# Delta-rule layer: tables by each head's half of the array, v kept on chip, and a scan that loads two chunks at a time

## The reference, cut to what matters

```python
r, k, v = heads(xr @ wr), heads(xk @ wk), heads(xv @ wv)
decay = heads(exp(-exp(w)))
kk = k * k_k;  kk = kk / max(norm(kk), 1e-12)
k = k * (1 + (a - 1) * k_a)
def step(S, (r_t, w_t, k_t, v_t, a_t, b_t)):        # a = -kk, b = kk * a
    sa = einsum('bhij,bhj->bhi', S, a_t)
    S = S * w_t + sa * b_t + v_t * k_t               # outer products over i, j
    return S, einsum('bhij,bhj->bhi', S, r_t)
S, y = scan(step, S0, ...)                           # S0: zeros (prompt), state_rwkv (stream)
y = groupnorm(y) * ln_w + ln_b + sum(r * k * r_k) * v    # the last term: the "bonus"
```

## Time and profile before

| | us |
|---|---|
| median of 3 runs | 4401.09 (4398.41 to 4402.56) |
| execution profiled, its own time | 4410.82 |
| its span | 4409.1 |
| TensorE busy (share of the span) | 3709.2 (84%) |
| VectorE busy | 1550.3 (35%) |
| ScalarE busy | 1213.5 (28%) |
| GpSimd busy | 573.6 (13%) |

### The profile page before, as it was taken

How to read it: one execution, slowest core, us unless ns; L and a number is a source line. 1 busy time by engine, 2 the same in 40 slices (tenths; PEclk the granted TensorE clock), 3 DMA queues, 4 the chain that set the end, 5 groups by cost and what they waited for, 6 DMA issues and landing times. The chain is left out here.

```text
span 4409.1 us, 58432 instructions
## 1 busy us (share of the span) xinstructions
PE 3709.2 (84%) x24411; PEld 3469.6 (79%) x24411; DVE 1550.3 (35%) x2413; ACT 1213.5 (28%) x2151; POOL 573.6 (13%) x812
## 2 busy tenths in 40 slices
PE   4889473699799999998978979387498699999998
PEld 3689361498699999998567969377398599999998
DVE  3310133532433223233414654554532333223233
ACT  2421223430232112122523432165330232112123
POOL 0000030010011001012202123433010021001011
PEclk7989686899899999999889988699799899999999
DMA  3322201012121111111544554587412211111111
GB/s 111 130 82 68 89 14 42 13 53 97 46 57 44 48 45 47 48 43 39 193 142 135 188 162 130 134 163 132 96 48 92 59 40 47 49 44 48 47 43 62
DMA packets 546227, 349.26 MB, mean 79 GB/s; under 512 B 244294, under 2 KB 509414, under 8 KB 542550
## 3 DMA queue, kind: packets, MB, share of 16 engines
q1 hardware_dynamic: 539830, 328.31, 26.4%
q0 software_dynamic: 6144, 17.34, 1.2%
HBM read 246.82 MB, written 98.85 MB: 78 GB/s over the span
## 5 line engine op out<-in xcount | busy, mean ns | idle before, releaser
L79 PE MATMUL ps<-ff_h,ff_wh 128*128 128x352 f32 x4224 | 1009.6, 322 | 0.0
L79 PEld LDWEIGHTS ps<-ff_h,ff_wh 128*128 128x128 f32 x4224 | 731.4, 188 | 1.3
L79 PE MATMUL ps<-y_parts,ff_wh 128*128 128x352 f32 x2880 | 702.7, 326 | 16.3 <-DVE ff_wl L1512 16.3
L79 PE MATMUL ps<-ff_h,ff_wl 128*128 128x352 f32 x2112 | 677.6, 321 | 0.0
L79 PEld LDWEIGHTS ps<-y_parts,ff_wh 128*128 128x128 f32 x2880 | 506.8, 190 | 16.6 <-DVE ff_wl L1512 16.6
L79 PE MATMUL ps<-y_parts,ff_wl 128*128 128x352 f32 x1440 | 469.3, 326 | 0.0
L79 PEld LDWEIGHTS ps<-ff_h,ff_wl 128*128 128x128 f32 x2112 | 396.4, 188 | 0.0
L79 PE MATMUL ps<-rw_parts,tb_wh 128*128 128x352 f32 (+1 forms) x1152 | 298.6, 342 | 82.0 <-DVE tb_wl L1512 28.2
L1656 DVE TENSOR_TENSOR x<-ps,x 128x352 f32<-128x352 f32 x240 | 126.0, 525 | 495.7 <-PE ps L79 493.1
L1889 POOL TENSOR_TENSOR ff_silu<-ff_silu,rs 128x352 f32<-128x352 f32 x132 | 126.3, 958 | 1234.8 <-ACT ff_silu L1828 1234.8
L79 PEld LDWEIGHTS ps<-rw_parts,tb_wh 128*128 128x128 f32 x1152 | 210.5, 199 | 92.4 <-DVE tb_st L2718 29.0
(11 more groups left out here) (407 smaller groups left out, 5859.4 us busy)
## 6 DMA issues: line engine op xcount, KB each, us to landing
ff_w<-in_ffn_w SPq DMA_DIRECT2D x120, 512.0 KB, 3.8
mixed_t<-oq_st SPq DMA_DIRECT2D x48, 176.0 KB, 1.8
rw_ra_d<-tb_ra SPq DMA_DIRECT2D x8, 1056.0 KB, 6.6
rw_kbt_d<-tb_kbt SPq DMA_DIRECT2D x8, 1056.0 KB, 3.9
rw_gg_d<-tb_gs SPq DMA_DIRECT2D x8, 1056.0 KB, 5.5
mk_w<-in_xa_wk SPq DMA_DIRECT2D x4, 2048.0 KB, 9.0
mk_w<-in_xa_wv SPq DMA_DIRECT2D x4, 2048.0 KB, 9.4
oq_w<-in_xa_wq SPq DMA_DIRECT2D x16, 512.0 KB, 4.1
```

The costliest lines, as they stand in the source:

```text
L79: mm = nc.tensor.matmul(out, l, part, start=start and n == 0, stop=stop and n == 2)
```

## The change

Tables:
- The weights' buffers (`Groups`) are made outside of both stages. SyncE loads units 0 and 1 in `low_ranks`, ScalarE rounds them after `bend_g(0)`, VectorE makes the low parts at the end. `low_ranks` has five stage slots instead of six and one buffer `low` instead of two.
- `kb` has 64 columns instead of 128: no zeroed copies. Each cross product is made twice, for the partitions 0 to 63 and 64 to 127 as rows and outputs, with the weights' 64 columns. `turn` does the same with `V`, which lies whole in SBUF, two pairs deep; `eye2` goes.
- `bonus` is one operation from V in SBUF for a whole pair, a step later, and TensorE doesn't wait for it. `beta` is loaded pair by pair.
- The ring of mixed tiles has ten places (`RING`).
- DRAM layouts of triangles and of v follow the heads' halves; v is stored in four copies a pair.

Scan: one block for prompt and stream, the stream's chunk first, all eight pairs in one piece for each operation. A load brings two chunks; kbt, v and tt are used as loaded; only g and ra are opened (four operations). x comes back behind the second load.

```diff
+RING = 10
     def cross(p, i):
-                for k in range(c0, c1):
-                    mm = nc.tensor.matmul(ps[:, 6, (k - c0) * HD:(k - c0 + 1) * HD], kb[:, k, :], eye2[:], start=True,
-                                          stop=True)
+                for k in range(c0, c1):
+                    for r in (slice(0, HD), slice(HD, P)):
+                        mm = nc.tensor.matmul(ps[r, 6, (k - c0) * HD:(k - c0 + 1) * HD], kb[r, k, :], ident[r, r],
+                                              start=True, stop=True)
...
-            def open_kb(q, which, of):
-                for h in range(2):
-                    nc.vector.scalar_tensor_tensor(out=kb[:, :, (2 * which + h) * C:(2 * which + h + 1) * C], in0=by_c(of),
-                                                   scalar=of_key[:, h:h + 1], in1=by_c(ei), op0=ALU.mult, op1=ALU.mult)\
-                        .then_inc(kb_done, 1)
+            def grown_key(which, of):
+                nc.vector.tensor_tensor(kb[:, :, which * C:(which + 1) * C], by_c(of), by_c(ei), ALU.mult)\
+                    .then_inc(kb_done, 1)
...
-                    if u >= 1:
-                        pe.wait_ge(bonus_done, 4 * (u - 1) + (1, 2, 4)[b])
                     groups.sum(pe, j, b, parts, 0, KT // 2)
...
+            def bonus(u):
+                dve.wait_ge(beta_in[u % 2], 32 * (u // 2 + 1))
+                dve.wait_ge(bonus_out, 16 * u)
+                for b in range(BLOCKS):
+                    groups.wait_emptied(dve, 2 * KT + u, b)
+                nc.vector.tensor_tensor(extra, V[:, u % 2], A[:, u % 2], ALU.mult).then_inc(bonus_done, 1)
...
+                if u >= 1:
+                    bonus(u - 1)
+                for _ in range(min(8, C - 1 - done) if 2 <= u < 6 else 8 if u >= 6 else 0):
+                    substitute(dve, nc.vector, 0, 0, share, done // (C - 1), done % (C - 1))
```

SyncE's side of the new scan:

```diff
+            sp.wait_ge(cleared, 2)
+            for l in range(NPC // 2 + 1):
+                if l >= 2:
+                    sp.wait_ge(y_done, last(l - 2) + 1)
+                w = 2 if l else 1
+                c = 2 * (l - 1) if l else NPC
+                s, got = l % 2, two_in[l % 2]
+                for t, d in ((g_in, g_d), (ra_in, ra_d), (kbt, kbt_d)):
+                    sp.dma_start(t[:, s, :, 0:w, :], d[:, :, c:c + w, :].rearrange("p r c x -> r p c x")).then_inc(got, 16)
+                for h in range(2):
+                    sp.dma_start(v[h * HD:h * HD + C, s, :, 0:w, :],
+                                 vt_d[:, h * C:(h + 1) * C, c:c + w, :].rearrange("p s c x -> s p c x")).then_inc(got, 16)
+                for q in range(2):
+                    for h in range(2):
+                        for odd in range(2):
+                            r = odd * HD + h * C
+                            for sub in range(w):
+                                sp.dma_start(tt[r:r + C, s, sub, 2 * q:2 * q + 2, h, C:HD],
+                                             tt_d[q, c + sub, h, odd].rearrange("p s t -> s p t")).then_inc(got, 16)
+                if l == 1:
+                    sp.dma_start(x[:], x_d.rearrange("(k p) t -> p k t", p=P)).then_inc(x_in, 16)
```

TensorE's (chunk n is half `sub` of load `l`; `last(l)` = 2 l):

```diff
+            def open_z(n):
+                (l, sub), s = two(n), n % 2
+                pe.wait_ge(opened, OPENS * (n + 1))
+                if n >= 2:
+                    pe.wait_ge(z_out, n - 1)
+                z_part(n, lambda p: g[:, s, p, 0], lambda p: v[:, l % 2, p, sub, :], True)
...
+                z_part(n, lambda p: ra[:, s, p, 0], lambda p: S[:, p, :], False).then_inc(z_done, 1)
+                y_part(n, lambda p: S[:, p, :], lambda p: ra[:, s, p, 1], True)
+                pe.wait_ge(z_out, n + 1)
...
+                        mm = nc.tensor.matmul(ps[side[h], 2 + p % 2, at:at + HD], tt[r, l % 2, sub, p // 2, h, :],
+                                              z[r, p // 2, :], start=True, stop=True)
+                mm.then_inc(u_done, 1)
+                if n + 1 < N:
+                    open_z(n + 1)
+                pe.wait_ge(u_out, n + 1)
...
+                        mm = nc.tensor.matmul(ps[r, 4, at:at + HD], kbt[r, l % 2, p, sub, :], vu[r, p, :],
+                                              start=True, stop=True)
+                mm.then_inc(s_done, 1)
+                y_part(n, lambda p: vu[:, p, :], lambda p: g[:, s, p, 1], False).then_inc(y_done, 1)
```

More of the change, by code:

```diff
@@ L552, in _, with delta_scan @@
             staggered(act, n, make, scan)
[L555 to L565, removed]
+def delta_scan(nc, ps, a, ra_d, g_d, kbt_d, vt_d, tt_d, dec, y, p_out, s_out, x, x_d, ident):
+    N = NPC + 1
     with ExitStack() as ctx:
[L567 to L584, removed]
@@ L587, in delta_scan @@
         end_turned, end_out, stored, x_in = sem("end_turned"), sem("end_out"), sem("stored"), sem("x_in")
-        LOADS, OPENS, FILLS = 8, 6, 3
+        OPENS = 4
         block = ctx.enter_context(nc.Block())
[L591 to L599, removed]
@@ L603, in _ @@
+        by_pair = lambda t: t.rearrange("i p (h j) -> i (p h) j", h=2)
         @block.sync
         def _(sp):
[L605 to L616, removed]
-                for h in range(2):
-                    for q in range(2):
-                        sp.dma_start(tt_in[h * C:(h + 1) * C, s, 4 * q:4 * q + 4, :],
-                                     tt_d[q, cc, h].rearrange("p s t -> s p t")).then_inc(chunk_in[s], 16)
@@ L622, in _ @@
[L622 to L630, removed]
+            sp.dma_start(of_head[:], a["c_heads"][1]).then_inc(heads_in, 16)
+            sp.dma_start(by_pair(turned[:, 0]), a["state_rwkv"][0, 0].rearrange("h i j -> i h j")).then_inc(init_in, 16)
@@ L658, in chunk @@
[L658 to L698, removed]
-                                              start=True, stop=True)
[L700 to L712, removed]
@@ L714, in _ @@
-            each(pe, chunk)
-            pe.wait_ge(state_ready, 2 * n + 2)
-            for p in range(PAIRS):
-                mm = nc.tensor.transpose(ps[0:HD, 2 + p // 4, p % 4 * P:p % 4 * P + P], state[:, p, :], ident[:])
-            mm.then_inc(end_turned, 1)
+            pe.wait_ge(init_in, 16)
+            for p in range(PAIRS):
+                mm = nc.tensor.transpose(ps[:, 7, p * HD:(p + 1) * HD], turned[:, 0, p, :], ident[0:HD, 0:HD])
+            mm.then_inc(init_turned, 1)
+            side = (slice(0, HD), slice(HD, P))
@@ L786, in _, with open_out @@
-            empty(n - 1)
+            act.wait_ge(heads_in, 16)
+            def open_out(n):
+                l, sub = two(n)
+                act.wait_ge(two_in[l % 2], due(l))
+                if n >= 2:
+                    act.wait_ge(y_done, n - 1)
+                for t, src in ((g, g_in), (ra, ra_in)):
+                    for h in range(2):
+                        nc.scalar.activation(t[:, n % 2, :, :, h], src[:, l % 2, :, sub, :]
+                                             .rearrange("r p (a t) -> r p a t", a=2), ACT.Copy, scale=of_head[:, h:h + 1])\
+                            .then_inc(opened, 1)
@@ L789, in gla_prep, with empty @@
+            def empty(n):
+                act.wait_ge(y_done, n + 1)
+                nc.scalar.activation(y[:, :, chunk(n) * C:(chunk(n) + 1) * C],
+                                     ps[:, 6 + n % 2, 0:4 * HD].rearrange("p (a t) -> p a t", a=PAIRS), ACT.Copy)\
+                    .then_inc(y_out, 1)
+            open_out(0)
+            for n in range(N):
+                if n + 1 < N:
+                    open_out(n + 1)
+                empty(n)
 def gla_prep(nc, ab, gate, qh, kh, v, dec, keep_d, heads_d):
@@ L2187, in _ @@
                 mix(n)
+            weights.low(dve, 0)
+            weights.low(dve, 1)
         @block.gpsimd
@@ L2374, in _ @@
                         sp.dma_start(R, pair_rows(r_d, q + 1)).then_inc(r_in, 16)
+                    else:
+                        load_beta(sp, 1)
                 if u >= 0:
```

356 lines of the change are left out of this document (173 added, 183 removed).

## The result

The changed kernel takes 4423.8 us (median of 5 runs, 4414.6 to 4426.7) against 4401.1 (5 runs, 4396.5 to 4406.1) on the same chip: a ratio of 1.0050 with a 95% interval of 1.0036 to 1.0065, which is 22.7 us more. The forecast was 36 more, 4437, in a range of 4350 to 4505: the sign holds, and the size is 13 us too high.

A forecast was written before the change was run, and what follows sets the result against it. It took TensorE as full in the tables' key steps, VectorE and DMA as setting their end, and TensorE and SyncE's queue as nearly full in the scan. Tables 104 us less, scan 140 more: 36 more, 4437, range 4350 to 4505.

The forecast's parts named there:

- Weights, ring, kb: Tables: weights loaded and split a stage earlier, 6.8 us less; ten-tile ring, 16 less; kb in two operations, 2.5 less.
- Cross products: Tables, key steps: 64 by 64 products alternating between halves save 5.8 us in each of eight steps, 46 us.
- Tiles of v: Tables: with ten ring tiles there when the keys end, the waits at v's tiles shrink by 10 us (0 to 15).
- Bonus and triangles: Tables: no TensorE wait on the bonus and less half clock, 19 us less; triangles asked for earlier, 4 less (-5 to 8).
- Substitution keeps its length: End of tables: the VectorE and DMA chain moves as a block with its start, same 127 us, iterations and bonus adding nothing.
- The scan: Scan: waits make loads run one after another, 22.6 us a period of two chunks; 397 us against 256.7, 140 more.
- Cheap small issues: Rival, scan: tt issues at 0.46 us and TensorE warm, period 17.5, 41 us less in all, 4360; chance 0.12.
- the turning point of 20.2: Scan: the period in us at about which the forecast total turns between slower and faster than before.
- Loads hidden: Rival, scan: loads run ahead, two chunks set the pace at 11.4 us, scan 229, total 4269; chance 0.10.
- Halves not side by side: Rival, tables: quadrants don't run in parallel, 16.5 us a pair instead of 8.3, tables only 39 less, 4502; chance 0.12.
- The ends of the tables' sum, 80 and 118: Tables: the forecast's range, in us less, around its sum of 104, for alternating halves.

The follow-up runs named there:

- the run with halves apart: Changed kernel with each cross product's two loops exchanged, all products of partitions 0 to 63 first, then 64 to 127: 4462.8 us, ratio 1.0134.
- the ring's run: Changed kernel with the ring of mixed tiles at 4 places instead of 10: 4449.0 us, ratio 1.0103.
- the run with all three edits of the scan: Changed kernel with 8 joined tt loads, g, ra and v first on their own semaphore, and open_z(n+1) behind y's last product: 4267.4 us, ratio 0.9687.
- the run with 28 idle products: Changed kernel with 28 unread identity products on TensorE where it would wait for the next load: 4429.9 us, ratio 1.0059.
- the run with early opening: Changed kernel with g, ra and v first in each load on their own semaphore, opening and open_z waiting for these alone: 4311.1 us, ratio 0.9790.

## Why the prediction was right, step by step

- **Weights, ring, kb: 6.8, 16 and 2.5.** From the tables' start the sums of the first keys came 133.4 us in before (2372.28 in its trace) and 109.7 after (2341.45), 23.7 less for the first two, against 22.8; the ring alone is 15.8 by its own run. The first cross, 153.9 and 127.7, gives kb its 2.5. TensorE's first product (2231.78) stands 0.04 us behind the stage's first issue, where it stood 6.9 behind, so the weights gave their 6.8.
- **Cross products: 46.** A key step takes 24.7 us against the forecast 24.6. The form that no row had shown took 0.061 us where the alternating scan products had given 0.063; the run with halves apart shows that alternating is what makes it so. The Trainium skill (TensorEngine Tiling, "Key Properties") has a change of the tiling mode drain TensorE; the sum left it out, and a step of 24.7 us leaves no room for the 4 us that it had been weighed at.
- **Tiles of v: 10.** The two stalls of 13.56 and 9.72 became 4.54 and 9.29, 9.4 less; the ring's run gives 8.4.
- **Bonus and triangles: 19 and 4.** Substitution starts 367.3 us in, where it was 473.1: 105.7 less, 104 forecast. Taking off the items above leaves some 24 for these two; they were not tried apart.
- **Substitution keeps its length: wrong by 5.6.** From 2599.08 to 2731.1 it is 132.0 us, before 126.4. The tables are 99.7 less and not 105 for that. The prediction had said that the iterations and the bonus add nothing, and on GpSimd, which does a share of each iteration beside VectorE, they do. Here is one of its operations, in the changed kernel and then in the kernel before:

```profile
2643.77 3.10 POOL L2289 TENSOR_TENSOR x<-x 88x192 f32<-88x192 f32 x1
...
2754.52 0.79 POOL L2319 TENSOR_TENSOR x<-x 88x192 f32<-88x192 f32 x1
```

Beside the first VectorE splits weights (1.21 us) and then makes the new bonus (1.24) out of two tiles in SBUF; the operation is 2.3 us longer. Before, an operation beside a split took 1.85 us, and the bonus, which read PSUM and one tile, lengthened none visibly. All six bonus products within the two substitutions show it, with 2.0 to 3.4 us for the GpSimd operation beside them, and its 124 operations take 98.2 us instead of 91.1. GpSimd ends the first half 57.4 us after its start, 2.4 behind VectorE, where both had been done after 53.1. This is read from the traces; no run takes the bonus away.

- **The scan: the mechanism as forecast, the period mis-sized.** Issue 13.3 (forecast 13.9), landing 1.3 (1.8), opening 2.6 (2.7), TensorE 4.1 (4.2): 21.2 instead of 22.6. Fifteen times 1.4 is 21 us, and the scan fell short of 397 by 20; the ends were not exact either, but nearly cancel (32 us and not 38 ahead of the third load, of which 4 came back behind the load of x, and 22 instead of 19 behind the last period). Of the 1.4, 0.6 is issue and 0.5 landing: a tt copy takes 0.545 where the sum took 0.62, kbt's price, though its own row of four tt copies gives 0.59.
- **The rivals.** Cheap small issues: 0.545 lies between the 0.46 of that rival and the 0.62 of the forecast, and the period stayed above the turning point of 20.2. Loads hidden: no, but the run with all three edits of the scan gets below the 229 that it named, with 222. Halves not side by side: no.
- **How much was luck.** The sign turned at a period of 20.2 and the period came at 21.2, so the side was held by 1 us a period. And two errors offset each other in part: 4 us less gained in the tables, 20 less lost in the scan. The ends of the tables' sum, 80 and 118, don't follow from the ranges given for its terms, which make 85 and 113.

The Trainium skill's rule on small transfers (DMA: Bandwidth & Descriptors, "Rules for kernel authors") pointed the right way: joining them gave 52 us, though by 3.8 us of issue a load. Its 2 us a transfer is the page's fit for transfers that GpSimd issues ("Anatomy of one DMA — SWDGE (gpsimd) path"); these are SyncE's, and as a sum it doesn't show: sixteen were issued in 8.7 us and the last had landed 1.3 later.

## What to carry to other kernels

When buffers are reused, look for what stands ahead of the releasing instruction on its own engine: here the y product that frees the buffer was queued behind a product that needs the next load, and double buffering bought nothing. Give the operands that are needed first their own transfers and their own semaphore, and put the release ahead of the next wait. Count the issues of a load by their measured time and set the sum beside the compute of the same stretch.

## What the hardware showed that I had not expected

- Beside idle products the same 21 issues took 14.1 and 14.4 us instead of 13.3, with nothing added to the queue.
- With half the tt issues the mean from the last issue to the opening rose from 1.3 to 2.2 us, and issue and landing together hardly varied (11.4 to 12.2 us) while issue alone went from 8.2 to 10.4: with that many issues, how fast the queue issues no longer decides alone.
- In the run with 28 idle products all three groups ran at full clock after one wait of 3.22 us; in the run with early opening they began at half clock after one of 2.19 us (1.12 and 1.97 us). Ahead of both the granted clock was 1.00. A pause's length alone doesn't tell which it will be.
- 64 by 64 products in one half alone were 0.117 us apart, in alternating halves 0.061.
- A GpSimd operation of 0.8 us lasted 3.1 where VectorE's split of weights and its product of two tiles in SBUF (1.21 and 1.24 us) ran beside it.
